# Hybrid attention encoder on one core: the softmax division moved from the weights to the gate, and transposes and value products issued two groups at a time

## What is computed

```python
p = jax.nn.softmax(s, axis=-1)                        # A: 8 heads, 2 key heads, top-256 keys of an indexer
e / (jnp.sum(e, axis=-1, keepdims=True) + jnp.exp(sk - m))   # B: 4 heads, window, with a sink
p = jax.nn.softmax(s, axis=-1)                        # M: 4 heads over 256 memory tokens
y = jnp.concatenate([o_a, o_b, o_m], axis=-1) * jax.nn.silu(gate)
x = x + jnp.einsum('btm,md->btd', y, w_out_l)
```

## Time and profile before

| what | value |
|---|---|
| median of 3 runs | 1,703.4 us (1,702.95 to 1,703.66) |
| the profiled execution's own time | 1,698.95 us |
| its span, first to last instruction | 1,697.2 us |
| mean granted TensorE clock | 0.939 |
| PE / VectorE / ScalarE / GpSimd busy | 92 / 61 / 39 / 7% |
| attention stage of one layer | 446 to 843 us, and again 1,272 to 1,669 us |

### The profile page before, as it was taken

One profiled execution on the slowest core, in us unless ns is written; L12 is line 12 of the kernel. 1 busy time (PEld: TensorE's weight loads), 2 busy tenths in 40 slices (PEclk: granted clock), 3 DMA queues, 4 the chain that ended last, 5 costly groups with the idle time before them and its releaser, 6 DMA issues. The chain is left out here.

```text
span 1697.2 us, 19595 instructions
## 1 busy us (share of the span) xinstructions
PE 1561.7 (92%) x6364; PEld 828.4 (49%) x6364; DVE 1028.4 (61%) x2685; ACT 660.1 (39%) x1628; POOL 118.8 (7%) x155
## 2 busy tenths in 40 slices
PE   2999999999889999999779999999997999999992
PEld 1544456666544444444444445566664444444451
DVE  0444526887667778767224453488766677777752
ACT  1223426775533323333112242477664333334332
POOL 0100013300000000000001001131000000000003
PEclk9999799999899999999679997999997999999976
DMA  7111310210411111010051004002004111111005
GB/s 270 53 40 33 132 45 1 84 54 39 173 40 37 38 38 38 1 38 19 24 185 50 24 22 146 25 1 112 40 38 162 38 38 38 38 38 38 20 1 232
DMA packets 80956, 105.22 MB, mean 62 GB/s; under 512 B 18864, under 2 KB 57488, under 8 KB 80784
## 3 DMA queue, kind: packets, MB, share of 16 engines
q1 hardware_dynamic: 80864, 104.04, 17.7%
HBM read 78.48 MB, written 29.97 MB: 64 GB/s over the span
## 5 line engine op out<-in xcount | busy, mean ns | idle before, releaser
L656 PE MATMUL score_ps<-w_slot,hT 128*128 128x512 f32 (+2 forms) x1024 | 388.6, 538 | 5.5 <-DMA w_slot<-in_w_in_dram 5.0
L656 PEld LDWEIGHTS score_ps<-w_slot,hT 128*128 128x128 f32 x1024 | 195.9, 194 | 186.3 <-issue 180.2
L1014 ACT ACTIVATE hT<-hT,neg_top 128x128 f32<-128x128 f32 (+8 forms) x144 | 118.1, 820 | 380.3 <-DVE neg_top L1263 380.1
L656 PE MATMUL score_ps<-w_slot,work 128*128 128x512 f32 x512 | 236.7, 617 | 0.5 <-ACT prob_bm L1027 0.5
L1158 DVE TENSOR_SCALAR_CACHE_REDUCE work<-bias,trial 128x384 f32<-128x384 f32 (+3 forms) x256 | 226.0, 883 | 6.9
L881 ACT ACTIVATE work<-bias,neg_trial 128x768 bf16<-128x768 f32 (+2 forms) x192 | 198.4, 1043 | 67.3 <-DVE neg_trial L1154 67.3
L786 PE MATMUL score_ps<-akT,query_mem 64*128 64x512 f32 (+4 forms) x448 | 194.7, 553 | 13.7 <-ACT prob_bm L1027 6.7
L656 PEld LDWEIGHTS score_ps<-w_slot,work 128*128 128x128 f32 x512 | 97.9, 196 | 124.8 <-issue 124.5
L1254 DVE CUSTOM_DVE_ANT_0 hT<-score_ps,bias 128x128 f32<-128x128 f32 (+8 forms) x144 | 115.7, 804 | 34.8 <-PE score_ps L786 33.9
L727 PE MATMUL score_ps<-hT,w_slot 128*128 128x352 f32 x448 | 135.2, 460 | 1.4 <-ACT gate_raw L1003 1.4
L786 PEld LDWEIGHTS score_ps<-akT,query_mem 64*128 64x128 f32 (+1 forms) x448 | 71.9, 185 | 114.0 <-issue 93.2
(11 more groups left out here) (174 smaller groups left out, 1777.1 us busy)
## 6 DMA issues: line engine op xcount, KB each, us to landing
gate_raw<-x_scratch SPq DMA_DIRECT2D x32, 512.0 KB, 3.7
w_slot<-in_w_in_dram SPq DMA_DIRECT2D x8, 2048.0 KB, 9.4
gate_scratch<-gate_raw SPq DMA_DIRECT2D x16, 528.0 KB, 2.7
w_slot<-in_w_out_dram SPq DMA_DIRECT2D x4, 2048.0 KB, 11.1
work<-gate_scratch SPq DMA_DIRECT2D x16, 512.0 KB, 4.7
x_scratch<-gate_raw SPq DMA_DIRECT2D x16, 512.0 KB, 2.6
hT<-x_scratch SPq DMA_DIRECT2D x8, 512.0 KB, 8.0
out_dram<-hT SPq DMA_DIRECT2D x8, 512.0 KB, 4.6
```

The lines of the kernel that those rows point to most:

```text
L656: last = nc.tensor.matmul(out[:, 0:cols], lhs(k), w[:, k, 0:cols], start=(k == 0), stop=(k == KD - 1))
L1014: nc.scalar.activation(p, p, ACT.Exp, bias=neg_b[0:r, j:j + 1], scale=SM_SCALE, accum_out=sums[t % 2][0:r, cols]).then_inc(prob_done, 1)
```

## The change

Two edits to the attention stage.

Division. The per-head `SCALE` is gone; PE's `PT` waits for the exps themselves. A new `SCALE` per tile and half (bm: B and M; a: A0 and A1) takes the reciprocal of eight sums at once, [rows, 8]. SP stores them to a scratch in HBM, one row of 128 per head, waits for it, and loads each row back, broadcast over the 64 partitions that hold the head's features (`norm_turn`). A new step `GATE_SCALE` on POOL multiplies the gate of that half by it, and `MIX` waits for that instead of for the gate's load. On SP the two `norm_turn` of tile t now come first, then the store of x(t-1), then the load for t+1. That makes 18 `SCALE` and 18 `GATE_SCALE` steps a layer, two per tile.

Pairs. A `PT` is held until a second one is there; both are then issued together, and behind them the two `PV` of the pair before. `prob_t` has four buffers instead of three. Of the 112 groups of a layer, this makes the order (here from tile 5's last groups to tile 6)

```diff
@@ attention_steps
-    steps += [("EXTRA",)] + [s for q in score_steps(1) for s in (q, ("SCALE",) + q[1:])]
+    def divisors(q):
+        t, kind, kv = ITEMS[q[1]]
+        done = kind == "M" or (kind == "A" and kv == 1 and q[2] == 3)
+        return [("SCALE", t, int(kind == "M")), ("GATE_SCALE", t, int(kind == "M"))] if done else []
+    steps += [("EXTRA",)] + score_steps(1)
+    waiting += divisors(score_steps(1)[-1])
...
-            steps.append(("PT", i, g))
-            if len(late) == 2:
-                steps += finish()
-            if g == 0 and waiting:
-                steps.append(waiting.pop())
-
-            waiting += [s for s in scale if ITEMS[s[1]][1] != "A"]
-            steps += [s for s in scale if ITEMS[s[1]][1] == "A"]
-            late.append(("PV", i, g))
+            held.append(("PT", i, g))
+            if len(held) == 2 or (i, g) == last_group:
+                steps += held
+                while late:
+                    steps += finish()
+                late += [("PV",) + s[1:] for s in held]
+                held.clear()
+            if g == 0:
+                steps += waiting
+                waiting.clear()
+            waiting += made
@@ SP
+                    def norm_turn(t, bm):
+                        r, rows = ROWS[t], norm_dram[t % 2, bm, :, 0:ROWS[t]]
+                        sp.wait_ge(inv_made[bm], t + 1)
+                        with nc.allow_non_contiguous_dma("a head's sums lie one to a partition"):
+                            sp.dma_start(rows.rearrange("c q -> q c"), inv_sum[t % 2][0:r, 8 * bm:8 * bm + 8]
+                                         ).then_inc(norm_written[bm], 16)
+                        sp.wait_ge(norm_written[bm], 16 * (t + 1))
+                        if t:
+                            sp.wait_ge(gate_scaled[bm], t)
+                        for u in range(2):
+                            src = rows[4 * u:4 * u + 4, :].rearrange("(a k) q -> a k q", a=1)
+                            sp.dma_start(norm_sb[HD * u:HD * (u + 1), 4 * bm:4 * bm + 4, 0:r],
+                                         src.broadcast_to([HD, 4, r])).then_inc(norm_loaded[bm], 16)
...
                     tile_load(0)
-                    for t in range(TILES):
-                        if t + 1 < TILES:
-                            tile_load(t + 1)
+                    tile_load(1)
+                    for t in range(TILES):
+                        norm_turn(t, 1)
+                        norm_turn(t, 0)
+                        if t:
+                            x_store(t - 1)
+                            if t + 1 < TILES:
+                                tile_load(t + 1)
+                    x_store(SMP)
@@ PE, PT
-                                pe.wait_ge(prob_scaled, SCALE_STEPS.index((i, len(score_steps(i)) - 1)) + 1)
+                                probs_written(pe, i, len(score_steps(i)) - 1)
@@ POOL
+                        elif kind == "GATE_SCALE":
+                            t, bm = step[1:]
+                            r, k = ROWS[t], slice(4 * bm, 4 * bm + 4)
+                            pool.wait_ge(gate_loaded[t % 2], 16 * (t // 2 + 1))
+                            pool.wait_ge(norm_loaded[bm], 32 * (t + 1))
+                            nc.gpsimd.tensor_tensor(gate_sb[t % 2][:, k, 0:r], gate_sb[t % 2][:, k, 0:r],
+                                                    norm_sb[:, k, 0:r], ALU.mult).then_inc(gate_scaled[bm], 1)
@@ VectorE, SCALE
-                            i, j = step[1:]
-                            t, what, _ = ITEMS[i]
-                            r, b, at, w = ROWS[t], t % 2, sum_cols(i, j), keys_of(ITEMS[i])
-                            probs_written(dve, i, j)
...
-                            link(nc.vector.reciprocal(inv_sum[b][0:r, at], sums[b][0:r, at]))
-                            if what == "A":
-                                p = item_buffers(i)[0][0:r, 1056 * j:1056 * j + w]
-                                ins = nc.vector.tensor_scalar(p, p, inv_sum[b][0:r, at], None, ALU.mult)
...
+                            t, bm = step[1:]
+                            r, b = ROWS[t], t % 2
+                            for i in [ITEMS.index((t, k, 0)) for k in "BM"] if bm else [ITEMS.index((t, "A", 1))]:
+                                probs_written(dve, i, len(score_steps(i)) - 1)
...
+                            if t >= 2:
+                                dve.wait_ge(norm_written[bm], 16 * (t - 1))
+                            at = slice(8 * bm, 8 * bm + 8)
+                            nc.vector.reciprocal(inv_sum[b][0:r, at], sums[b][0:r, at]).then_inc(inv_made[bm], 1)
@@ VectorE, MIX
-                            dve.wait_ge(gate_loaded[b], 16 * (t // 2 + 1))
+                            dve.wait_ge(gate_scaled[bm], t + 1)
```

More of the change, by code:

```diff
@@ L92, in attention_steps @@
 def attention_steps():
-    steps, late, waiting = [], [], []
+    steps, late, waiting, held = [], [], [], []
+    last_group = (len(ITEMS) - 1, len(groups_of(ITEMS[-1])) - 1)
     def finish():
@@ L108, in finish @@
         return out
-    steps += [("EXTRA",)] + [s for q in score_steps(1) for s in (q, ("SCALE",) + q[1:])]
+    def divisors(q):
[4 more added lines that the diff above has]
+    waiting += divisors(score_steps(1)[-1])
     for i, it in enumerate(ITEMS):
-        if waiting and waiting[0][1] == i:
-            steps.append(waiting.pop())
         nxt = score_steps(i + 2) if i + 2 < len(ITEMS) else []
@@ L124, in attention_steps @@
                 steps.append(("ADD", t - 1, c))
-            scale = []
+            made = []
             while given < len(nxt) and given * groups <= g * len(nxt):
-                steps += [nxt[given]] + scale
-                scale = [("SCALE",) + nxt[given][1:]]
+                steps.append(nxt[given])
+                made += divisors(nxt[given])
                 given += 1
@@ L131, in attention_steps @@
                 for q in nxt[given:]:
-                    steps += [q] + scale
-                    scale = [("SCALE",) + q[1:]]
-            steps.append(("PT", i, g))
-            if len(late) == 2:
-                steps += finish()
-            if g == 0 and waiting:
-                steps.append(waiting.pop())
-            waiting += [s for s in scale if ITEMS[s[1]][1] != "A"]
-            steps += [s for s in scale if ITEMS[s[1]][1] == "A"]
-            late.append(("PV", i, g))
+                    steps.append(q)
+                    made += divisors(q)
+            held.append(("PT", i, g))
[9 more added lines that the diff above has]
+            waiting += made
     while late:
@@ L177, in plan @@
         if f == KD - 1:
-            steps += [("QK", 0, 0), ("SCALE", 0, 0)]
+            steps += [("QK", 0, 0)]
         steps.append(("GATE", f))
@@ L215 @@
 QK_STEPS = [s[1:] for s in STEPS if s[0] == "QK"]
-SCALE_STEPS = [s[1:] for s in STEPS if s[0] == "SCALE"]
 def copied_by_dve(a):
@@ L299, in hybrid_stream_kernel @@
         relu_sb = [work[:, 1056 * b:1056 * (b + 1)] for b in range(2)]
-        prob_t = [work[:, 2112 + 512 * b:2624 + 512 * b] for b in range(3)]
+        prob_t = [work[:, 2112 + 512 * b:2624 + 512 * b] for b in range(3)] + [sb("prob_t3", [P, 512])[:, :]]
         gate_sb = [work[:, 3648 + 1024 * b:4672 + 1024 * b].rearrange("p (k n) -> p k n", k=KD) for b in range(2)]
@@ L363, in hybrid_stream_kernel @@
         pv_done = sem("pv_done")
-        prob_scaled = sem("prob_scaled")
+        inv_made = [sem(f"inv_made_{s}") for s in ("a", "bm")]
+        norm_written = [sem(f"norm_written_{s}") for s in ("a", "bm")]
+        norm_loaded = [sem(f"norm_loaded_{s}") for s in ("a", "bm")]
+        gate_scaled = [sem(f"gate_scaled_{s}") for s in ("a", "bm")]
         mixed_bm = sem("mixed_bm")
@@ L419, in sum_cols @@
             kind, g = ITEMS[i][1:]
-            return slice(4 * g + j, 4 * g + j + 1) if kind == "A" else slice(8, 12) if kind == "B" else slice(12, 16)
+            if kind == "A":
+                head = 4 * g + j
+                return 4 * (head % 2) + head // 2
+            return 8 + 4 * (j // 2) + j % 2 + (0 if kind == "B" else 2)
         def gate_banks(f):
@@ L1025, in _ @@
                             for slot in range(4):
-                                at, col = slice(256 * slot, 256 * slot + w), cols.start + slot
+                                at, col = slice(256 * slot, 256 * slot + w), sum_cols(i, slot)
                                 ins = nc.scalar.activation(prob[0:r, at], ps[0:r, at] if direct else prob[0:r, at],
@@ L1035, in _ @@
                             bank, free = turned(step)
-                            if a >= 3:
-                                act.wait_ge(pv_done, a - 2)
-                            nc.scalar.copy(prob_t[a % 3][0:w, 0:n], bank.rearrange("p k n -> p (k n)")[0:w, 0:n]).then_inc(free, 1)
+                            if a >= 4:
+                                act.wait_ge(pv_done, a - 3)
```

(8 more changed lines are left out.)

29 lines of the change are left out of this document (14 added, 15 removed).

## The result

| | before | after |
|---|---|---|
| median beside each other | 1,703.2 us | 1,683.2 us |
| ratio, 95% interval | | 0.9913 (0.9888 to 0.9938) |
| profiled execution's time | 1,698.95 us | 1,682.72 us |
| its span, granted clock | 1,697.2 us, 0.939 | 1,680.9 us, 0.941 |

The account below looks back on a forecast made before the run. TensorE's own pace was taken as the attention stage's bound. Pairing's 18.4 us less 1.3 of net waits and 1.5 in tile 0 gave 15.6 a layer, 31 in all: 1,672 us from 1,703.4, range 1,648 to 1,704.

Parts of the forecast that it names:

- Pairing, 18.4 us: Attention: like groups in succession save TensorE 0.15 us at 111 places, 0.19 at nine score places; 18.4 us a layer.
- Waits removed, 7.8 us: Attention: TensorE's waits that go, 6.5 us for ScalarE's copies and 1.3 of the score waits a layer.
- New waits of heads and gated products, 9.1 us: Tile heads wait for copies behind exps, 5.5 us a layer; OUT waits for the gated product, 3.6.
- The port, priced at nothing: POOL's 36 products could hold VectorE up to 47 us through a shared port; nothing added to the sum.
- Rival B: New waits cost TensorE's clock, 1.6 us at six more places, 9.6 us a layer: 1,691 us; chance 0.14.
- Tile 0, priced at nothing: Tile 0 lacks cover; half A's product ends near 478 us, so it ends no sooner and 1.5 us of pairs buy nothing.
- The way after tile 0: Divisors' way through HBM, about 8.5 us (bounds 6 and 18), under 18 us of cover: costs nothing from tile 1 on.
- signs of being wrong: Wrong if eights take twice 0.59 us, TensorE's waits in a layer exceed 20, or the store lands later than 10.
- A: VectorE's relief removes TensorE's waits and heads wait for nothing: 27.2 us a layer, 1,649 us; chance 0.12.
- C: Pairing brings nothing, as semaphores rather than changes of kind cost time: 1,706 us, no change; chance 0.07.
- D: At each head both transpose banks wait behind two sets of exps: 16 us lost a layer, 1,735 us; chance 0.08.
- E: Divisor arrives after its cover in every tile; with slowest landings a 27 us way, 1,834 us; chance 0.02.

Follow-up runs that it names:

- division alone (7): The two-stores kernel with the order of before, one transpose group and one value group at a time, without pairing: 1,682.9 us, ratio 0.9920.
- pairing alone (1): The kernel before with only the paired order and fourth buffer; VectorE still scales each head, nothing goes through HBM: 1,712.3 us, ratio 1.0064.
- Experiment 9: The kernel with tile 0 divided in place, plus VectorE copying the two groups behind each memory head's score: 1,630.0 us, ratio 0.9595.
- two-stores kernel: The changed kernel, with both of tile 0's divisor stores issued before the wait for the first: 1,659.1 us, ratio 0.9750.
- experiments 5 and 10: One program, the changed kernel with tile 0 divided in place, run and later repeated in more rounds: 1,644.9 us, then 1,641.8 us.
- Experiment 8: The two-stores kernel, with half A's divisors stored twice in series from tile 1 on: 1,715.8 us, ratio 1.0107.
- experiment 5: The changed kernel, with tile 0 alone divided in place by VectorE as before, no divisor through HBM: 1,644.9 us, ratio 0.9710.
- Experiment 3: The changed kernel, with both of tile 0's divisor stores issued ahead of the first wait; the same run as the two-stores kernel: 1,659.1 us, ratio 0.9750.
- experiment 4: The changed kernel, its store writing each row's eight divisors as one 32-byte run (result wrong, work the same): 1,657.7 us, ratio 0.9738.

## Why the prediction was right in direction and wrong in size

The account for the stretch after tile 0, layer 0, from the windows above (idle is the length less PE's busy time):

| | length | PE busy | idle |
|---|---|---|---|
| before | 347.2 | 338.1 | 9.1 |
| division alone (7) | 333.8 | 332.8 | 1.0 |
| pairing alone (1) | 358.2 | 329.4 | 28.8 |
| both (after) | 326.3 | 316.1 | 10.2 |

Layer 1 gives PE busy times of 338.1, 332.8, 326.7 and 316.1 us and idle times of 9.1, 1.0, 28.9 and 10.3.

- **Pairing, 18.4 us with 1.5 of it in tile 0, so 16.9 after it:** 332.8 - 316.1 = 16.7 us from division alone to both. This term was right, and so were 0.15 us a place (0.155 in the rows) and the bounds chosen for two value groups (0.10 to 0.19). Some 2 us of the 16.7 are clock, an estimate: PE stands at 1.2 GHz for 19.8 us of the one stretch and 15.7 of the other.
- **Waits removed, 7.8 us:** idle fell from 9.1 to 1.0, 8.1 us. Right.
- **New waits of heads and gated products, 9.1 us:** 10.2 - 1.0 = 9.2 us. Right in sum, though 1.0 of it is the port's (next), which was priced at nothing, and nearly in parts: the heads' waits for ScalarE's copies are 6.4 us for 5.5 (0.58 for 0.75 in tile 6), each `OUT` waits 0.41 us for 0.45. Experiment 9 shows the cause of the heads' part.
- **The port, priced at nothing:** the trace shows VectorE held beside POOL's product. In tile 3:

```profile
555.29 1.27 POOL L1110 TENSOR_TENSOR work<-work,norm_sb 128x512 f32<-128x512 f32 x1 [14.48 <-DMA norm_sb<-norm_scratch]
555.35 1.24 DVE L1336 TENSOR_SCALAR neg_top<-top 128x4 f32<-128x4 f32 x1
559.08 0.66 PE L682 MATMUL turn_ps<-ident,prob_bm 128*128 128x128 f32 x4 [1.95 <-ACT work L1080]
```

The negated maximum of the memory head takes 0.17 us elsewhere; here it takes 1.24 and ends 0.03 us after POOL. The four exps, the first copy and PE's transposes come later by as much: PE waits 1.95 us, where the two-stores kernel, in which POOL starts 0.16 us behind that instruction, waits 0.88. In layer 1 it is 1.16 and 1.87 us. Eight such holds cost VectorE 7.0 us over the two layers, not 47, but one a layer falls on a memory head and costs PE 1.0 us. It also parts experiments 5 and 10: at tile 2's head the same instruction takes 1.18 us in the first, and PE waits 2.10 us there for 1.08.
- **Not counted: what the clock gives back.** Division alone takes 5.3 us off PE's busy time with the same matmuls, in both layers. The granted clock rises from 0.95 to 0.97: before, PE ran at half speed (1.2 GHz) in three short stretches between tile 1 and tile 7, from 505.5, 594.2 and 689.8 us, 13.7 us in all; in division alone there is none between 493 and 806 us. They begin 0.2 to 1.3 us behind the end of waits of 1.34, 1.67 and 1.38 us (at 505.34, 592.89 and 689.29); these waits are gone. Rival B had the direction turned round: it priced what new waits cost the clock, and nothing in the prediction priced what removed ones give. Experiment 8 is the other direction: longer waits put in, 8.9 us more busy time. It is no rule for a single wait: before, the longest, 1.71 us at 640.08, has no such stretch behind it. The kernel after keeps one (3.4 us, from 559.8) behind its longest head wait, 1.95 us, in layer 0 and none behind the one of 1.87 us in layer 1.
- **Tile 0, priced at nothing beside pairs that buy nothing ("So tile 0 ends no sooner"):** this is the step that failed. Measured 12.0 us lost in layer 0 and 12.8 in layer 1, 24.8 in all, and by experiment 5 it also hid a gain of 4.9 and 4.2 us that the rest of the change brings to tile 0 (the pairs alone 3.5 and 3.6, experiment 7). Two things in it were wrong. First, the store was priced by the nearest row, a scattered load of as many elements that lands in 3.3 us; it landed in 10.3 (median; in tile 0 the loads follow the issue of their store by 13.5 and 8.9 us), and the loads of half M went out at 474.27 instead of some 470. Second, and larger, half A's product was put 3.5 us behind half M's (478 for 474.5), although SP waits for one store before it issues the next and the prediction's own way for a turn was 8.5 us. It came 11.5 us behind (489.25 for 477.78). With its own 8.5 the prediction would have had half A's product end near 483, and a loss of 5 us a layer. Experiment 3 takes the series away and gives 24 us back, 19.3 of them in tile 0. The bound of 18 us for the way was written down, but it entered the sum for the tiles with cover alone and not for the one without.
- **The way after tile 0:** "nothing, from tile 1 on" held, but closely. From SP's issue of half A's store (506.33) to the end of POOL's product (522.29) tile 1 takes 16.0 us, not 8.5; the gated product starts 2.2 us later. The cover of 18 us was sized well, the way was not.
- **The descriptor rule.** The Trainium skill (DMA: Bandwidth & Descriptors, rules for kernel authors) makes a non-contiguous last dimension one descriptor per element. The prediction set a load's row against it and took 3.3 us. The trace agrees with the rule: the kernel after moves 122,623 packets and experiment 4 93,055, and the 29,568 between them are just the elements less the pieces, 32 x (1,024 - 128) + 4 x (256 - 32). What the rule does not give is the price: a quarter of the elements 4.2 us, an eighth of the pieces 1.4.

Two of the prediction's own signs of being wrong came true: the store lands later than 10 us, and PE's waits in layer 0's attention are over 20 us (the first three rows of the list above are 28.9).

The rivals: A fell, the heads still wait. B fell in size; of its mechanism one stretch is left in layer 0. C fell by 16.7 us of busy time. D does not happen with both parts, and does with pairing alone. E did not happen from tile 1 on; its mechanism was the one that cost tile 0.

In sum, a layer after tile 0: 16.7 + 8.1 - 9.2 + 5.3 = 20.9 us for 15.6 forecast; tile 0 lost 12.4 on average for 0. That the time still lies in the range is partly luck, since a gain and a loss that were both left out stand against each other. Without tile 0's loss the profiled execution would stand at 1,682.7 - 24.8 = 1,658 us, 10 below the forecast for it; the two-stores kernel, whose tile 0 is still 3.3 and 2.2 us longer than before, came in at 1,659.

## What to carry to other kernels

When a wait is put on a serial queue, work out the case without cover (the first tile, the first pass) by itself and in series: each turn's whole way, times the turns. A removed engine's work and a reordering may each be worth nothing or less alone and a good deal together, so price them on the same chain. And a scattered store is not priced by a scattered load: count its elements.

## What the runs showed of the hardware that was not expected

- A store to HBM from 128 partitions in 4-byte elements takes 10.3 us for 1,024 of them and 4.2 for 256, where as many as 1,024 4-byte elements loaded (`gamma`, the same view of the kernel after) land in 2.7 and 3.4 us; as 32-byte pieces the same 4 KB take 1.4 us. Two such stores in flight together cost hardly more than one: the loads behind them go out 14.3 us after the first store's issue, for 13.5 behind one store (experiment 3).
- The issue of tile 0's first store occupied SP for 3.02 us in both layers; from the third on it took 0.32 to 0.37.
- Waits of 1.3 to 1.7 us of TensorE were followed by stretches at 1.2 GHz in three cases of four, and removing them came with 5.3 us a layer less busy time beside 8.1 us of waits; adding 16.5 us of waits cost 8.9 us of it (experiment 8).
- POOL's product of two SBUF tiles holds some VectorE instructions until it ends: in the kernel after eight small ones on SBUF (128x4 negated maxima, 0.17 us elsewhere, and the like) end 0.02 to 0.04 us after a product that was running when they began, up to 1.27 us long. It does not hold all: VectorE's reduction of a score bank in PSUM, begun at 594.90 with POOL busy from 594.38 to 595.67, takes 1.23 us, as it does at 518.84 with POOL idle. The Trainium skill (SBUF — State Buffer, SBUF: two separate sides) has the two engines share a port pair under an exclusive lock that is held for a whole instruction, against a VectorE instruction in a two-port mode or with two SBUF inputs; the trace agrees that the later one waits for the end of the other. Which instructions were in a two-port mode no run here shows.
